# Gathering an expert's tokens as quarter rows and turning them on VectorE instead of TensorE

## The chip, the cores and the metric

The kernel runs on one core of a Trainium2 chip. The metric is the device time of one execution in microseconds (us), as the median of the runs shown. The engines that matter here are TensorE (PE in the profile; PEld is its weight load), VectorE (DVE), ScalarE (ACT), GpSimd (POOL, whose queue issues the gathers), and SyncE (SP, whose queue issues the weight loads). All transfers run on the core's 16 DMA engines.

## The reference

Three layers on 512 tokens of 1024 features in fp32. The first is a gated linear attention mixer followed by a mixture of experts, the second a Fourier and attention layer, the third a recurrent (RG-LRU) layer. The change lies in the mixture of experts and in the step that prepares its input:

```python
h = modulate(rmsnorm(h, norm_mlp_w[l]), sh2, sc2)        # 512 tokens x 1024
logits = xt @ w_router + b_router                        # top 4 of 32 experts for each token
def expert_block(args):                                  # one expert's tokens at a time
    gu = xblk @ w_gu[e] + b_gu[e]                        # 1024 x 2048
    gate, up = jnp.split(gu, 2, axis=-1)
    gate = jnp.minimum(gate, SWIGLU_LIMIT)
    up = jnp.clip(up, -SWIGLU_LIMIT, SWIGLU_LIMIT)
    act = (up + 1.0) * gate * jax.nn.sigmoid(SWIGLU_ALPHA * gate)
    return act @ w_down[e] + b_down[e]                   # 1024 x 1024
```

## The kernel before

**The norm step.** For each of the four blocks of 128 tokens, VectorE writes the normalised rows to `xnt` (`normalise`, L1252), TensorE turns them for the router, and GpSimd's queue stores them as rows of 1024 features in DRAM (`xn_scratch`, L1202). ScalarE squares the rows, takes the root and modulates half of the turned block (`square`, `modulate`).

**The experts.** Experts run one after the other, each with room for 96 tokens (`CAP`). Weights come through a ring of 12 slots of 1 MiB in SBUF: 8 tiles of `w_gu` and 4 of `w_down` for each expert, 12 MiB. SyncE's queue issues a load as soon as the semaphore `used` says that TensorE has left the slot (L1540). TensorE computes in column groups of 32: `gate_up` (L1774) makes, for each of 8 weight tiles, 12 matmuls of 512 columns (three groups of 32 tokens by four quarters of the columns, each split in two instructions as fp32), and a last set of 12 for the bias in bf16. `down` (L1754, L1759) does the same for the second product, one expert late.

One pass of the loop, `block_step(e)`, does this on TensorE, in this order: `gate_up` of expert e, its bias matmuls, the turning of the gathered tokens of expert e + 1 (`pe_turn`, L1458, eight transposes from `xe` into PSUM), `down` of expert e - 1, and the four small matmuls of `pe_ids` (L1448) that make the row numbers of expert e + 3 from a one-hot matrix. There are 32 passes; the first has no `down`. The loop's other engines:

- VectorE: reads the row numbers into `idx` (`dve_ids`, L1441), makes the one-hot matrix of the expert after (`dve_onehot`, L1437), then, once the bias matmuls are done, gate, up, their product and the 32x32 block transpose of the result (L1644 to L1658).
- GpSimd: waits for the row numbers and for both halves of the turning (L1505), then issues the gather of the next expert (`pool_gather`, L1492): one indirect transfer of 96 rows of 4 KB into partitions 0 to 95 of `xe`. A row number that is out of bounds moves nothing.
- ScalarE: the sigmoid (L1588), then eight modulations from PSUM into `xeT` (`act_modulate`, L1499), then the copies of `down`'s result (L1598, L1600) and its stores to `y_scratch` (L1604, L1607).

`gate_up` of expert e + 1 waits for all eight modulations. Ahead of the loop stands a chain for the first expert: one-hot, `pe_ids`, `idx`, gather, turning, modulation. SyncE loads three copies of the bias to 32 partitions each (L1521), waits for the first gather and then issues the six weight loads that have slots (L1529).

A last block of code serves experts with over 96 tokens, from a list that the kernel makes (`extra_blocks`).

## Time and profile before

| | before |
|---|---|
| median of 3 runs | 2387.15 us (2386.14 to 2388.25) |
| the profiled execution's own time | 2389.86 us |
| its span in the trace | 2387.9 us |
| granted TensorE clock, mean over the span | 0.971 |
| the experts, from the first `gate_up` to the last `down` | 364.6 to 1424 us |

Times below are in us from the start of the span unless marked ns. "Share" of the DMA engines is the mean busy share of 16 engines and can be a little over 1, since packets overlap. In a group row, the number after x is the count of instructions; [idle before <-X] is the engine's idle time and what ended it.

### The profile page before, as it was taken

What the parts mean: (1) busy time and instruction counts of PE and PEld (TensorE: products, weight loads), DVE (VectorE), ACT (ScalarE), POOL (GpSimd) and SP (SyncE); (2) the same over time, 40 slices, a digit from 0 to 9 for tenths busy, and PEclk for the clock granted to TensorE, in tenths of its full rate; (3) what the DMA queues carried; (4) which work ended last, traced back from release to release, by engine and by line L of the source; (5) the groups of instructions that cost most, each with busy time, mean ns of one, the idle gap of its engine ahead of it and who ended that gap; (6) DMA issues with size and microseconds to landing.
All of it is one profiled execution on the core that took longest, in us unless ns stands there. A gap on an engine that the chain in (4) does not pass through costs nothing. (4 is left out here: it accounts for less than half of the span.)

```text
span 2387.9 us, 35818 instructions
## 1 busy us (share of the span) xinstructions
PE 2249.2 (94%) x14707; PEld 930.6 (39%) x14707; DVE 681.3 (29%) x1157; ACT 486.8 (20%) x908; POOL 68.3 (3%) x105
## 2 busy tenths in 40 slices
PE   5999878999999999999999982999999998999998
PEld 2434532333333333333333330446445444444443
DVE  1133446111111111111111116003067103365633
ACT  2121212111110111101111111110016102456530
POOL 0000000000000000000000003000000000000000
PEclk8999888999999999999999995999999999999999
DMA  9138429999999999999999954422210121222100
GB/s 357 53 124 314 183 102 375 389 404 397 400 412 399 402 396 401 408 406 399 400 399 406 409 208 152 159 71 85 85 71 1 53 71 44 71 88 88 71 36 35
DMA packets 142023, 556.62 MB, mean 233 GB/s; under 512 B 17433, under 2 KB 32946, under 8 KB 108082
## 3 DMA queue, kind: packets, MB, share of 16 engines
q1 hardware_dynamic: 118662, 512.67, 55.3%
q0 software_dynamic: 9520, 30.29, 3.8%
q10 hardware_dynamic: 13788, 12.93, 1.6%
q8 instruction: 36, 0.59, 0.1%
q14 instruction: 17, 0.14, 0.0%
HBM read 535.77 MB, written 25.03 MB: 235 GB/s over the span
## 5 line engine op out<-in xcount | busy, mean ns | idle before, releaser
L1774 PE MATMUL ps<-ring,xeT 128*32 128x512 f32 x6144 | 670.4, 596 | 5.2 <-ACT xeT L1499 5.2
L1774 PEld LDWEIGHTS ps<-ring,xeT 128*32 128x32 f32 x6144 | 197.0, 110 | 450.3 <-issue 448.2
L1754 PE MATMUL ps<-ring,aT 128*32 128x512 f32 x2048 | 267.5, 594 | 1.0 <-ACT ysb L1600 1.0
L1644 DVE TENSOR_SCALAR gate<-ps 128x768 f32<-128x768 f32 x32 | 30.6, 958 | 606.7 <-PE ps L1774 606.7
L1588 ACT ACTIVATE sig<-gate 128x768 f32<-128x768 f32 x32 | 27.0, 845 | 702.1 <-DVE gate L1644 702.1
L360 PE MATMUL ps<-hT_late,ring 128*128 128x512 f32 x384 | 165.2, 592 | 1.7 <-PEq L2000 1.7
L1759 PE MATMUL ps<-ring,aT 128*32 128x256 f32 x2048 | 157.6, 379 | 0.0
L1759 PEld LDWEIGHTS ps<-ring,aT 128*32 128x32 f32 x2048 | 67.0, 110 | 152.7 <-issue 152.7
L2687 PE MATMUL ps<-hT_late,ring 128*128 128x512 f32 x256 | 110.6, 592 | 1.7 <-PEq L2446 1.7
L360 PE MATMUL ps<-ring,mT 128*128 128x512 f32 x256 | 110.1, 592 | 1.2 <-PEq L2253 1.2
L2700 PE MATMUL ps<-hT_late,ring 128*128 128x512 f32 x256 | 110.5, 592 | 0.0
L2738 PE MATMUL ps<-ring,mT 128*128 128x512 f32 x256 | 110.2, 592 | 0.0
L360 PEld LDWEIGHTS ps<-hT_late,ring 128*128 128x128 f32 x384 | 72.9, 190 | 93.3 <-issue 93.3
L1658 DVE STREAM_TRANSPOSE aT<-up 128x768 f32<-128x768 f32 x32 | 31.3, 978 | 232.2 <-PE ps L1759 232.2
L1499 ACT ACTIVATE xeT<-ps,mod 128x96 f32<-128x96 f32 x264 | 88.1, 437 | 1.6 <-PE ps L1458 1.6
L360 PE MATMUL ps<-ring,hT_late 128*128 128x512 f32 x192 | 82.6, 592 | 1.2 <-PEq L2110 1.2
L1754 PEld LDWEIGHTS ps<-ring,aT 128*32 128x32 f32 x2048 | 63.7, 110 | 42.7 <-ACT ysb L1600 1.1
L360 PEld LDWEIGHTS ps<-ring,mT 128*128 128x128 f32 x256 | 48.6, 190 | 62.7 <-issue 62.7
L2687 PEld LDWEIGHTS ps<-hT_late,ring 128*128 128x128 f32 x256 | 48.6, 190 | 62.7 <-issue 62.7
L2738 PEld LDWEIGHTS ps<-ring,mT 128*128 128x128 f32 x256 | 48.6, 190 | 61.2 <-issue 61.2
L2700 PEld LDWEIGHTS ps<-hT_late,ring 128*128 128x128 f32 x256 | 48.6, 190 | 61.2 <-issue 61.2
L360 PE MATMUL ps<-ring,hT 128*128 128x512 f32 x160 | 71.7, 598 | 0.0
(364 smaller groups left out, 1959.7 us busy)
## 6 DMA issues: line engine op xcount, KB each, us to landing
ring<-in_w_gu SPq DMA_DIRECT2D x256, 1024.0 KB, 12.1
ring<-in_w_down SPq DMA_DIRECT2D x128, 1024.0 KB, 12.8
ring<-in_even_w_in SPq DMA_DIRECT2D x18, 1024.0 KB, 6.2
ring<-in_w_ada SPq DMA_DIRECT2D x32, 512.0 KB, 6.5
ring<-in_odd_w_in SPq DMA_DIRECT2D x32, 512.0 KB, 5.5
ring<-in_w_ada SPq DMA_DIRECT2D x8, 1024.0 KB, 20.7
ring<-in_w_in SPq DMA_DIRECT2D x8, 1024.0 KB, 15.6
y_scratch<-ysb ACTq DMA_DIRECT2D x128, 64.0 KB, 5.0
```

The lines of the kernel that those rows point to most:

```text
L360: mm = nc.tensor.matmul(dst, left(k, w, kk), right(k, w, kk), start=first, stop=last)
L1499: nc.scalar.activation(xeT[:, k, 0:tokens_], ps[:, 6 + k // 4, at:at + tokens_], ACT.Identity, bias=mod2[:, k, 0:1], scale=mod2[:, KD + k, ...
L1588: nc.scalar.activation(sig[:, 0:W], gate[:, 0:W], ACT.Sigmoid, scale=1.702).then_inc(M.sig_ready, 1)
L1644: nc.vector.tensor_scalar(thirds(gate[:]), part_banks(0), 7.0, None, ALU.min).then_inc(M.gu_read, 1)
L1658: nc.vector.transpose(turned[:, 0:W], up[:, 0:W]).then_inc(M.aT_read, 1)
L1754: mm = nc.tensor.matmul(quad(Y0, 2 * q + n), acted(k, q), w[:, kk, n * BANK:(n + 1) * BANK], start=first, stop=last)
L1759: mm = nc.tensor.matmul(quad(Y0 + 1, c, 256), acted(k, 2), w[:, kk, c * 256:(c + 1) * 256], start=first, stop=last)
L1774: mm = nc.tensor.matmul(quad(q, c), left(q), part_columns(w, c), start=start, stop=stop)
L2687: mm = nc.tensor.matmul(bank(j.bank), w[:, b * P:(b + 1) * P], hT[:, k, :], start=k == 0, stop=k == KD - 1)
L2700: mm = nc.tensor.matmul(bank(j.bank), w[:, 512 + b * P:512 + (b + 1) * P], hT[:, k, :], start=k == 0, stop=k == KD - 1)
L2738: return nc.tensor.matmul(bank(j.bank), mT[:, k, t * P:(t + 1) * P], w[:, k % 2, h * BANK:(h + 1) * BANK], start=k == 0, stop=k == 2 * KD - 1)
```

## The change

The step that turns an expert's tokens moves from TensorE to VectorE, and the gather is laid out for it. VectorE transposes within blocks of 32 partitions and 32 columns. So the tokens are gathered as quarters of rows: quarter r of the token in slot 32q + s goes to partition 32r + s, columns 256q to 256q + 255. That takes three indirect transfers for an expert (q = 0, 1, 2), each of 128 quarter rows of 1 KB, with three columns of row numbers. One VectorE transpose of 128x768 then gives features on partitions. For the weights' rows to stay in natural order, the normalised rows are stored in another feature order (j, r, f to r, j, f), by ScalarE, which now writes a second copy of them in the norm step (`spread`).

The row numbers need the slot within 32 (`place`) and the third that it lies in (`third_of`), made by three VectorE steps ahead of the loop; `pe_ids` multiplies by six columns instead of two, masked by the third (`mine`, four more VectorE steps for each expert), and `dve_ids` takes two VectorE steps instead of one. The transposes leave TensorE, and the `used` signal that the first of them gave is given by the first matmul of `down`, or by `pe_ids` in the first pass. The waits follow: GpSimd waits for VectorE's transpose, ScalarE modulates from SBUF. The block for experts with over 96 tokens is changed in the same way. The core of the diff:

```diff
             def _(pool):
                 posm_zero.on(nc.gpsimd.memset(posm[:], 0.0))
                 for t in range(NT):
-                    pool.wait_ge(xn2_ready.sem, t + 1)
-                    xn2_stored.on(pool.dma_start(xn_dram[t * P:(t + 1) * P, :], xnt[:, t, :]), 16)
+                    pool.wait_ge(xq_ready.sem, t + 1)
+                    xn2_stored.on(pool.dma_start(xn_dram[t * P:(t + 1) * P, :], xq[t]), 16)
                 xn2_stored.wait(pool)
...
+                def spread(t):
+                    act.wait_ge(n2_mean.sem, 2 * t + 2)
+                    xq_ready.on(nc.scalar.activation(xq[t].rearrange("p (q j f) -> p j q f", q=4, f=QUAD),
+                                                     res[:, t, :].rearrange("p (j q f) -> p j q f", q=4, f=QUAD), ACT.Copy,
+                                                     scale=stat[:, 4 + t:5 + t]))
...
                 for t in range(NT):
                     square(t)
+                    spread(t)
                     modulate(t)
...
-        xe = sbuf("xe", [P, D], scope=moe_scope)
+        W = 3 * FF * QUAD // P
+        DQ = D // 4
+        xe = sbuf("xe", [P, W], scope=moe_scope)
+        xturned = sbuf("xturned", [P, W], scope=moe_scope)
+        place, third_of = (sbuf(f"{name}_of", [P, NT, E + 3], scope=moe_scope) for name in ("place", "third"))
+        placex, thirdx = (sbuf(f"{name}_extra", [P, NT, XB], scope=moe_scope) for name in ("place", "third"))
...
-        tokens = sbuf("tokens", [P, NT, 2], BF16, scope=moe_scope)
-        W = 3 * FF * QUAD // P
+        tokens = sbuf("tokens", [P, NT, 6], BF16, scope=moe_scope)
+        mine = sbuf("mine", [P, NT, 6], BF16, scope=moe_scope)
+        row = sbuf("row", [P, 3], scope=moe_scope)
         Q2 = slice(BANK, W)
         sel = sbuf("sel", [3 * E, P], BF16, scope=moe_scope)
-        idx = sbuf("idx", [P, 1], U32, scope=moe_scope)
+        idx = sbuf("idx", [P, 3], U32, scope=moe_scope)
...
-        iota1 = cst[:, C_IOTA1:C_IOTA1 + P]
+        slots = cst[:, C_SLOT:C_SLOT + P]
+        row_moved = signal("row_moved")
         ident3 = cst[0:3 * E, C_ID3:C_ID3 + E + 1]
...
-        def dve_onehot(dve, S, pos):
+        def split_places(step, pos, place_, third_):
+            step(nc.vector.tensor_scalar(third_, pos, float(QUAD), None, ALU.is_gt))
+            step(nc.vector.scalar_tensor_tensor(out=third_, in0=pos, scalar=2.0 * QUAD, in1=third_, op0=ALU.is_gt, op1=ALU.add))
+            step(nc.vector.scalar_tensor_tensor(out=place_, in0=third_, scalar=-float(QUAD), in1=pos, op0=ALU.mult, op1=ALU.add))
+        def dve_onehot(dve, S, place_, third_):
             for t in range(NT):
-                ins = nc.vector.tensor_scalar(onehot[:, t, 0:CAP], iota1[:, 0:CAP], pos(t), None, ALU.is_equal)
+                nc.vector.tensor_scalar(onehot[:, t, :], slots, place_(t), None, ALU.is_equal)
+                ins = nc.vector.scalar_tensor_tensor(out=mine[:, t, :], in0=cst[:, C_THIRD:C_THIRD + 6], scalar=third_(t),
+                                                     in1=tokens[:, t, :], op0=ALU.is_equal, op1=ALU.mult)
             ins.then_inc(S.onehot_ready, 1)
-        def dve_ids(dve, S):
-            nc.vector.tensor_scalar(idx[:], ps[:, IDS, 0:1], ps[:, IDS, 1:2], float(NONE), ALU.add, ALU.add).then_inc(S.ids_read, 1)
+        def dve_ids(dve, S, n):
+            nc.vector.tensor_reduce(row[:], ps[:, IDS, 0:6].rearrange("p (q c) -> p q c", q=3), AX.X, ALU.add) \
+                .then_inc(row_moved.sem, 1)
+            dve.wait_ge(row_moved.sem, n)
+            nc.vector.tensor_scalar(idx[:], row[:], cst[:, C_ROW:C_ROW + 1], None, ALU.add).then_inc(S.ids_read, 1)
...
         def pe_ids(pe, S, first=None):
             for t in range(NT):
-                mm = nc.tensor.matmul(ps[:, IDS, 0:2], onehot[:, t, :], tokens[:, t, :],
+                mm = nc.tensor.matmul(ps[:, IDS, 0:6], onehot[:, t, :], mine[:, t, :],
                                       start=t == 0, stop=t == NT - 1)
...
+        quarter_rows = xn_dram.rearrange("t (q n) -> (t q) n", q=4)
         def pool_gather(pool, S):
-            nc.gpsimd.indirect_dma_start(xe[0:CAP, :], None, xn_dram, bass.IndirectOffsetOnAxis(ap=idx[0:CAP, :], axis=0),
-                                         bounds_check=T - 1, oob_is_err=False).then_inc(S.gathered, 16)
-        def act_modulate(act, S, tokens_=CAP):
-            for k in range(KD):
-                at = (k % 4) * P
-                nc.scalar.activation(xeT[:, k, 0:tokens_], ps[:, 6 + k // 4, at:at + tokens_], ACT.Identity,
-                                     bias=mod2[:, k, 0:1], scale=mod2[:, KD + k, 0:1]).then_inc(S.xeT_read, 1)
+            for q in range(3):
+                nc.gpsimd.indirect_dma_start(xe[:, q * DQ:(q + 1) * DQ], None, quarter_rows,
+                                             bass.IndirectOffsetOnAxis(ap=idx[:, q:q + 1], axis=0),
+                                             bounds_check=4 * T - 1, oob_is_err=False).then_inc(S.gathered, 16)
+        def dve_turn(S):
+            nc.vector.transpose(xturned[:], xe[:]).then_inc(S.xT_done, 1)
+        def act_modulate(act, S):
+            for j in range(KD):
+                nc.scalar.activation(xeT[:, j, 0:CAP].rearrange("p (q s) -> p q s", q=3),
+                                     xturned[:].rearrange("p (q j s) -> p j q s", q=3, j=KD)[:, j], ACT.Identity,
+                                     bias=mod2[:, j, 0:1], scale=mod2[:, KD + j, 0:1]).then_inc(S.xeT_read, 1)
...
                 for part in range(3):
                     bgu_loaded.on(sp.dma_start(bgu[part * E:(part + 1) * E, :], A["b_gu"][0]), 16)
-                sp.wait_ge(M.gathered, 16)
+                sp.wait_ge(M.gathered, 48)
...
             def _(pool):
                 nc.gpsimd.memset(mark[:], 0.0).then_inc(M.marked, 1)
                 amat_zero.on(nc.gpsimd.memset(xe[:], 0.0))
+                amat_zero.on(nc.gpsimd.memset(xeT[:, :, CAP:], 0.0))
                 amat_zero.wait(pool)
-                for e in range(2):
-                    pool.wait_ge(M.ids_read, e + 1)
-                    if e:
-                        pool.wait_ge(M.xT_done, 2)
-                    pool_gather(pool, M)
+                pool.wait_ge(M.ids_read, 1)
+                pool_gather(pool, M)
+                pool.wait_ge(M.ids_read, 2)
+                pool.wait_ge(M.xT_done, 1)
+                pool_gather(pool, M)
                 def block_step(e):
                     pool.wait_ge(M.ids_read, e + 3)
-                    pool.wait_ge(M.xT_done, e * 2 + 4)
+                    pool.wait_ge(M.xT_done, e + 2)
                     pass_on(pool, M, e + 1)
                     pool_gather(pool, M)
...
-                    act.wait_ge(M.xT_done, e * 2 + 4)
+                    act.wait_ge(M.xT_done, e + 2)
                     act_modulate(act, M)
...
-                rest.on(nc.vector.memset(onehot[:, :, CAP:], 0.0))
-                rest.on(nc.vector.tensor_copy(tokens[:].rearrange("p t c -> p (t c)"), cst[:, C_TOK:C_TOK + 2 * NT]))
+                def list_step(ins):
+                    listing.on(ins)
+                    listing.wait(dve)
+                split_places(list_step, posm[:], place[:], third_of[:])
+                for q in range(3):
+                    rest.on(nc.vector.tensor_copy(tokens[:, :, 2 * q:2 * q + 2],
+                                                  cst[:, C_TOK:C_TOK + 2 * NT].rearrange("p (t c) -> p t c", t=NT)))
                 rest.wait(dve)
                 for e in range(3):
                     if e:
                         dve.wait_ge(M.ids_done, e)
-                    dve_onehot(dve, M, lambda t: posm[:, t, e:e + 1])
+                    dve_onehot(dve, M, lambda t: place[:, t, e:e + 1], lambda t: third_of[:, t, e:e + 1])
                     if e < 2:
                         dve.wait_ge(M.ids_done, e + 1)
                         if e:
-                            dve.wait_ge(M.gathered, 16 * e)
-                        dve_ids(dve, M)
+                            dve.wait_ge(M.gathered, 48)
+                        dve_ids(dve, M, e + 1)
+                        if e:
+                            dve.wait_ge(amat_zero.sem, buffers_zero)
+                            dve_turn(M)
...
                 def block_step(e, first):
                     dve.wait_ge(M.ids_done, e + 3)
-                    dve.wait_ge(M.gathered, e * 16 + 32)
-                    dve_ids(dve, M)
-                    dve_onehot(dve, M, lambda t: posm[:, t, bass.ds(e + 3, 1)])
+                    dve.wait_ge(M.gathered, e * 48 + 96)
+                    dve_ids(dve, M, e + 3)
+                    dve.wait_ge(M.xeT_read, e * 8 + 8)
+                    dve_turn(M)
+                    dve_onehot(dve, M, lambda t: place[:, t, bass.ds(e + 3, 1)], lambda t: third_of[:, t, bass.ds(e + 3, 1)])
                     dve.wait_ge(M.gate_done, e + 1)
...
@@ -1737,11 +1785,8 @@
                     if e:
                         pe.wait_ge(M.ids_read, e)
                     pe_ids(pe, M)
-                    if e == 0:
-                        pe.wait_ge(M.gathered, 16)
-                        pe_turn(pe, M.xT_done, xe, tokens_=CAP)
-                def down(e, m0, turn):
+                def down(e, m0, turn, final=False):
...
                             for q, n in pair_units():
                                 mm = nc.tensor.matmul(quad(Y0, 2 * q + n), acted(k, q), w[:, kk, n * BANK:(n + 1) * BANK],
                                                       start=first, stop=last)
+                                if first and q == n == 0 and not final:
+                                    mm.then_inc(stream.used, 1)
                             if last:
...
@@ -1787,18 +1835,16 @@
                         parted.wait(pe)
                     pe.wait_ge(M.sel_ready, e + 1)
                     gate_up(lambda q: sel[:, 0:QUAD], bparts[:], False, True).then_inc(M.gate_done, 1)
-                    pe.wait_ge(M.gathered, e * 16 + 32)
-                    pe_turn(pe, M.xT_done, xe, first=stream.used, tokens_=CAP)
                     if not first:
                         down(e, m0 + 8, turn)
                     pe.wait_ge(M.onehot_ready, e + 4)
                     pe.wait_ge(M.ids_read, e + 3)
-                    pe_ids(pe, M, first=None if first else stream.used)
+                    pe_ids(pe, M, first=stream.used)
...
-    cst[:, C_IOTA1:C_IOTA1 + P] = j + 1
+    cst[:, C_SLOT:C_SLOT + P] = j % 32 + 1
     cst[:, C_TRI:C_TRI + P] = p < j
...
     for t in range(NT):
-        cst[:, C_TOK + 2 * t:C_TOK + 2 * t + 1] = p
-        cst[:, C_TOK + 2 * t + 1] = P * t - NONE
+        cst[:, C_TOK + 2 * t:C_TOK + 2 * t + 1] = 4 * p
+        cst[:, C_TOK + 2 * t + 1] = 4 * (P * t - NONE)
     cst[:, C_RESET:C_RESET + T + TC] = np.arange(T + TC) % CHUNK != 0
     cst[:, C_XI:C_XI + XB] = np.arange(XB)
+    cst[:, C_THIRD:C_THIRD + 6] = np.arange(6) // 2
+    cst[:, C_ROW:C_ROW + 1] = 4 * NONE + p // 32
```


## Rows read from the trace of the kernel before

**Rows 1.** The page: busy time, mean ns of one, idle before.
```profile
PE 2249.2 (94%) x14707; PEld 930.6 (39%) x14707; DVE 681.3 (29%) x1157; ACT 486.8 (20%) x908; POOL 68.3 (3%) x105
...
L1658 DVE STREAM_TRANSPOSE aT<-up 128x768 f32<-128x768 f32 x32 | 31.3, 978 | 232.2 <-PE ps L1759 232.2
```

**Rows 2.** Windows in the experts: busy by engine, PEclk, DMA share, GB/s.
```profile
500.00:600.00 100.00, 100.00 (x1052) 34.64 (x1048) 16.92 (x33) 12.88 (x33) 3.48 (x6) 1.00 1.01 400
...
1200.00:1300.00 100.00, 100.00 (x1052) 34.61 (x1044) 16.91 (x33) 12.88 (x33) 3.47 (x6) 1.00 1.02 403
```

**Rows 3.** Timeline of TensorE around one pass: start us, us, instructions.
```profile
909.34 0.88 PE L1458 MATMUL ps<-cst,xe 96*128 96x96 f32 x8
910.15 1.06 PE L1754 MATMUL ps<-ring,aT 128*32 128x512 f32 x8
...
920.61 0.25 PE L1448 MATMUL ps<-tokens,onehot 128*128 128x2 bf16 x4
...
942.18 0.88 PE L1458 MATMUL ps<-cst,xe 96*128 96x96 f32 x8
```

**Rows 4.** DMA issues, us to landing: 394:400, 500:600, 1250:1350.
```profile
ring<-in_w_gu SPq DMA_DIRECT2D x1, 1024.0 KB, 6.7
...
ring<-in_w_gu SPq DMA_DIRECT2D x24, 1024.0 KB, 8.9
...
ring<-in_w_gu SPq DMA_DIRECT2D x24, 1024.0 KB, 15.0
```

**Rows 5.** Windows of one pass: while its gather's packets move, and the rest.
```profile
915.00:920.00 5.00, 5.00 (x68) 1.98 (x64) 0.00 (x0) 0.00 (x0) 0.00 (x0) 1.00 1.02 309
920.00:948.00 28.00, 28.00 (x292) 9.50 (x288) 5.63 (x11) 4.29 (x11) 1.15 (x2) 1.00 1.02 418
```

**Rows 6.** DMA, ten passes (900 to 1228.4): packets, MB, share of 16 engines.
```profile
q10 hardware_dynamic: 3840, 3.94, 3.4%
q0 software_dynamic: 1120, 2.83, 2.9%
...
xe<-xn_scratch,idx POOLq DMA_INDIRECT x10, 8.8
```

**Rows 7.** Windows elsewhere: bias loads, input loads, gathers of the next stage.
```profile
355.00:357.00 2.00, 0.16 (x4) 0.07 (x3) 0.94 (x5) 0.00 (x0) 0.61 (x1) 0.50 1.02 217
10.00:14.00 4.00, 0.00 (x0) 0.00 (x0) 0.00 (x0) 1.28 (x1) 0.00 (x0) 1.00 1.02 392
...
1440.00:1443.00 3.00, 3.00 (x4) 1.15 (x4) 0.75 (x1) 0.00 (x0) 0.00 (x0) 0.50 0.97 399
```

**Rows 8.** Timeline ahead of the first gate_up: the chain of the first expert.
```profile
354.03 0.81 DVE L1437 TENSOR_SCALAR onehot<-cst,posm 128x96 bf16<-128x96 f32 x4
...
355.20 0.22 DVE L1441 TENSOR_SCALAR idx<-ps 128x1 uint32<-128x1 f32 x1 [0.36 <-PE ps L1448]
...
356.39 1.02 POOL L1492 DMA_INDIRECT xe<-xn_scratch,idx  x1 [2.43 <-DVE idx L1441]
...
360.30 1.54 PE L1458 MATMUL ps<-cst,xe 96*128 96x96 f32 x8 [5.14 <-DMA xe<-xn_scratch,idx]
...
361.88 2.68 ACT L1499 ACTIVATE xeT<-ps,mod 128x96 f32<-128x96 f32 x8 [1.55 <-PE ps L1458]
...
377.35 0.29 DVE L1689 SCALAR_TENSOR_TENSOR sgT<-cst,sgT 128x128 f32<-128x128 f32 x1
```

**Rows 9.** Timeline, later: start of the second expert, and ScalarE in one pass.
```profile
393.65 0.64 PE L1774 MATMUL ps<-ring,xeT 128*32 128x512 f32 x4 [3.81 <-ACT xeT L1499]
...
911.19 2.67 ACT L1499 ACTIVATE xeT<-ps,mod 128x96 f32<-128x96 f32 x8
```

**Rows 10.** Timeline of the norm step, last block: ScalarE and VectorE.
```profile
341.10 1.06 ACT L1211 ACTIVATE kT<-res 128x1024 f32<-128x1024 f32 x1 [8.49 <-DVE res L1243]
...
345.33 1.50 ACT L1219 ACTIVATE ring<-ps,mod 128x128 f32<-128x128 f32 x4 [2.19 <-PE ps L1342]
```

**Rows 11.** The instructions on the tile idx: ns min/median/max, first and last start.
```profile
L1492 POOL DMA_INDIRECT xe<-xn_scratch,idx x34: 966/971/1025, 356.4 to 1403.7; - x34
```

More of the change, by code:

```diff
@@ L426, in build @@
         posm = sbuf("posm", [P, NT, E + 3])
-        posx = sbuf("posx", [P, NT, XB])
         wk = sbuf("wk", [P, NT, TOPK])
@@ L1122, in build @@
         parts = kT[:].rearrange("p a n -> p (a n)")[:, D:D + T]
+        xq = [a.rearrange("p h n -> p (h n)") for a in (vtok[:, 0:2, :], vtok[:, 2:4, :], vtok[:, 4:6, :], ptok[:, 0:2, :])]
         rt = sgT[:].rearrange("p h n -> p (h n)")
@@ L1188, in build @@
         posm_zero = signal("posm_zero")
+        xq_ready = signal("xq_ready")
         with nc.Block() as block:
@@ L1452, in pe_ids, with pe_turn @@
             mm.then_inc(S.ids_done, 1)
-        def pe_turn(pe, signal_, src, first=None, n=KD, tokens_=P):
-            for k in range(n):
-                at = (k % 4) * P
-                mm = nc.tensor.transpose(ps[:, 6 + k // 4, at:at + tokens_], src[0:tokens_, k * P:(k + 1) * P],
-                                         ident[0:tokens_, 0:tokens_])
-                if k == 0 and first:
+        def pe_turn(pe, signal_, src, first):
+            for k in range(KD):
+                mm = nc.tensor.transpose(ps[:, 6 + k // 4, (k % 4) * P:(k % 4 + 1) * P], src[:, k * P:(k + 1) * P], ident)
+                if k == 0:
                     mm.then_inc(first, 1)
-                if k % 4 == 3 or k == n - 1:
+                if k % 4 == 3:
                     mm.then_inc(signal_, 1)
@@ L1658, in block_step @@
                     nc.vector.transpose(turned[:, 0:W], up[:, 0:W]).then_inc(M.aT_read, 1)
-                def step(ins):
-                    listing.on(ins)
-                    listing.wait(dve)
+                step = list_step
                 def weights_and_rows():
@@ L1717, in _ @@
                 listing.wait(dve)
-                step(nc.vector.tensor_reduce(posx[:], indw, AX.X, ALU.add))
+                posx = ind.rearrange("p x e -> p (x e)")[:, 0:NT * XB].rearrange("p (t x) -> p t x", t=NT)
+                step(nc.vector.tensor_reduce(posx, indw, AX.X, ALU.add))
                 step(nc.vector.scalar_tensor_tensor(
-                    out=posx[:], in0=xval[:, 1:2, :].to_broadcast([P, NT, XB]), scalar=-float(CAP), in1=posx[:],
+                    out=posx, in0=xval[:, 1:2, :].to_broadcast([P, NT, XB]), scalar=-float(CAP), in1=posx,
                     op0=ALU.mult, op1=ALU.add))
+                split_places(step, posx, placex[:], thirdx[:])
                 step(nc.vector.tensor_copy(xlist[:, 0:XB], xval[:, 0, :]))
@@ L1800, in _ @@
                     block_step(i + 1, 8, i, False)
-                down(E, 8 + 12 * (E - 1), 0)
+                down(E, 8 + 12 * (E - 1), 0, final=True)
                 stream.taken = end_moe
@@ L1911, in body @@
                     pe.wait_ge(X.act_ready, i + 1)
-                    pe_turn(pe, X.aT_done, up, first=x_used)
+                    pe_turn(pe, X.aT_done, up, x_used)
                     pe.wait_ge(X.aT_read, i * 2 + 2)
```

24 lines of the change are left out of this document (12 added, 12 removed).

## The prediction

> **What bounds the kernel now.** I read the page first. TensorE is busy for 2249 us of the span, every other engine for under a third of it [rows 1]. The windows of 100 us inside the experts say more: TensorE is busy for all of each window at full granted clock, and at the same time the 16 DMA engines have a share of 1.01 to 1.02 and move 400 to 403 GB/s [rows 2]. So there are two candidates for the bound, and the first question is which of them ends last in a pass of the expert loop.
>
> The timeline of one pass answers it for TensorE [rows 3]: from one turning (909.34) to the next (942.18) is 32.84 us, and the queue of matmuls has no hole. The landing times of the weight loads answer it for the DMA [rows 4]: a load takes 6.7 us from issue to landing at the start of the loop, 8.9 us around 550, 15.0 us around 1300. The DMA engines are therefore late by a little more after each pass (6.1 us in 750 us, or 22.8 passes: 0.27 us a pass), and nothing waits for them, because the ring absorbs it. A slot that is left is needed again eleven twelfths of a pass later, 30.1 us, and 15.0 is well below that. TensorE is the bound, the DMA engines stand right behind it. What is taken from TensorE can be had only as far as the ring has room.
>
> What a pass asks of the DMA engines, in parts: twelve loads of 1 MiB are 12.58 MB, the stores 3.94 MB in ten passes, together 12.98 MB [rows 6]. Between gathers the core moves 418 GB/s [rows 5], so this takes 31.04 us. The gather is 0.283 MB a pass [rows 6] (about 69 rows of 4 KB), 0.68 us at that rate. But while its packets move, for about 5 us, the core moves only 309 GB/s [rows 5]: 5 x (418 - 309) / 418 = 1.30 us more are lost. The sum, 33.02 us against a pass of 32.84, agrees with the lag of 0.27 to within 0.1. So the gather is dear less for its bytes than for what it does to the others while it runs.
>
> **The change, part by part.**
>
> *The transposes leave TensorE.* From the first transpose to the first matmul of `down` is 910.15 - 909.34 = 0.81 us [rows 3]. The bound from the other side is the group's busy time, 0.88. The matmul behind it waits for things done long before. In the first pass nothing is gained: TensorE then idles 3.81 us for the modulations [rows 9], whose chain starts at the bias matmuls, not at the turning. 31 passes remain: 31 x 0.81 = 25.1 us less (up to 27.3). The new pass is 32.03 us.
>
> *`pe_ids` with six columns for two.* Four matmuls take 0.25 us with two columns [rows 3]; four more columns each are priced at nothing (at most 31 x 0.1 = 3 us, if every small matmul grew by 25 ns).
>
> *VectorE's additions in a pass*: a transpose of 128x768 (0.98 us [rows 1]), four small masks, one small reduction (each about `idx`'s 0.22 [rows 8]), some 2.1 us. VectorE is under a fifth busy [rows 2], and these stand right behind `pe_ids`, 20 us ahead of the next bias matmuls that VectorE waits for. Nothing on the path. Behind them on VectorE stands only the one-hot matrix, which TensorE wants 30 us later.
>
> *GpSimd*: three gathers of about 1.0 us issue time instead of one. They can be issued some 4 us after `pe_ids`, where the old one was issued after the turning, and they are needed at the next `idx`, 30 us later: 3 us of issue and 8.8 us of landing [rows 6] leave 17 us. Without that cover each us would cost 31.
>
> *ScalarE* modulates from SBUF; the eight took 2.67 us and ended at 913.9 [rows 9], 6.9 us ahead of the next `gate_up` (920.8, right behind `pe_ids` [rows 3]). It stays covered, with 0.8 less. Exposed it is only for the first two experts; a different price from SBUF would show there, within 1 us.
>
> *The norm step*: a copy of 128x1024 on ScalarE for each block of tokens, priced by the square of the same size, 1.06 us [rows 10]. It fits in the 2.19 us in which ScalarE waits for TensorE's turning. Zero; at most 1 us if the spread access pattern doubled it.
>
> *The chain of the first expert* is exposed, and it grows [rows 8]. Added: three steps of 128x140 ahead of the one-hot (0.29 each for 128x128, with hand-overs 1.0); two more small copies (0.4); four masks beside the one-hots, which take 0.81 for four (0.4); the reduction and its wait (0.3); two more gathers issued one after the other (2 x 1.02, with gaps 2.3). Taken away: TensorE's turning of 1.54 for VectorE's 0.98 (-0.5). Sum +3.9, taken as +4; bounds 3 and 6 (all small steps at 0.3, and hand-overs doubled). The six loads behind the first gather (L1529) start as much later, but so does TensorE's demand for them.
>
> *The gathers on the DMA engines* is the part that the trace does not show. Bytes stay 0.283 MB; in packets of 1 KB they cost at most what the stores of 1 and 2 KB rows cost, 3.94 MB in 3.4% of 16 x 328.4 us, that is 353 GB/s [rows 6]: 0.80 us. The disturbance is the open term, between 0 and three times 1.30. What makes it? A queue of GpSimd's beside SyncE's is not enough: at 10 to 14, GpSimd's loads of the input rows run beside weight loads, into all 128 partitions, at 392 GB/s. Into few partitions it is different: the bias loads, 32 partitions each, run at 217 GB/s at a share of 1.02, with no gather beside them at 355. And gathers of 128 rows, alone, run at 399 [rows 7]. The old gather fills at most 96 partitions, mostly the lowest 69; the new ones go to all 128. So I take the value near 0: a pass then asks 31.04 + 0.80 = 31.84 us of the DMA engines, just under 32.03, and the lag no longer grows.
>
> The Trainium skill, DMA: Bandwidth & Descriptors, The descriptor swizzle, says that in a transfer over 128 partitions each engine's writes go to the partitions behind one port of its own, and the same page's Back-pressure in remote DMA that a saturated port holds up the engines behind it (told there for transfers between cores). Our two windows at 217 and 392 GB/s are what that would look like; that it explains the gather's 309 no row shows. By it the disturbance would be 0, and the sum the one I give.
>
> **Sum.** -25.1 + 4 = -21.1 us. The profiled execution has a span of 2387.9 and a time of 2389.86; it would give 2368.8. From the median of the runs, 2387.15, comes 2366.
>
> **How much of the lag is free.** At the start a load lands in 6.7 us [rows 4]; with the shorter pass the limit is 29.4. So 22.7 us of lag can grow over 31 passes before TensorE waits: a pass may ask 32.03 + 0.73 of the DMA engines. If it asks g us more than 32.03, the loop gets 31g - 22.7 longer. All of the gain is gone at 31g = 22.7 + 21.1, g = 1.41: a disturbance of 32.03 + 1.41 - 31.84 = 1.60 us a pass, barely more than the old one.
>
> **The rivals.**
>
> *A, the disturbance stays 1.30.* It goes with the bytes or with the mixture of scattered rows, not with the partitions. For it: the old gather's cost is real and its cause not proven. Against: the loads at 10 to 14. A pass asks 33.14 of the DMA, g = 1.11, 34.4 - 22.7 = 11.7 us are given back as waits of `gate_up` and `down` for weight tiles in the last third of the loop. Time 2366 + 12 = 2378.
>
> *B, slower: each of the three transfers disturbs as the one did.* The place is the loop, the mechanism a cost for each indirect transfer or for each of its row numbers (384 for 96). For it: a dip of 5 us for 0.3 MB looks like something other than bytes. Against: GpSimd's direct loads, which have as many packets. At three times, 3.90, g = 3.71 and 115 - 22.7 = 92 us come back: 2458. At twice, 2.60, g = 2.41: 52 us, 2418. It decides from 1.60 on, 0.53 for each transfer.
>
> The Trainium skill, DMA: Bandwidth & Descriptors, Anatomy of one DMA and Rules for kernel authors, speaks against the change here: a transfer has some 2.0 us fixed, and many small ones should be made one. Were these 2.0 us time of the DMA engines, two more transfers would ask 4.0 us more a pass, an estimate from that page, and by it beside A's 1.30 g would be 5.1 and the time near 2502. The windows speak for latency instead.
>
> *C, another small mishap*: the first expert's chain at its upper bound together with a gather or a modulation that is late in some passes, 5 to 15 us given back: 2371 to 2381. The gathers run only for the 32 experts: 34 issues [rows 11], two of them ahead of the loop, so the block for over 96 tokens does not run.
>
> **How the numbers follow.** The forecast 0.60, A 0.15, B 0.18, C 0.07. The forecast's own range is 2361 (0.88 for each turning, a chain of 3) to 2371. The range for 8 in 10 takes in A and C, and the start of B, where the disturbance lies between 1.3 and 1.9: 2360 to 2394. What a measurement can tell from no change here is 0.2%, 4.8 us: same is 2382.4 to 2391.9, which lies between A and B. So faster 0.75 (the forecast, most of A and C), same 0.06, slower 0.19.
>
> **What would show it.** In the timeline of a pass `down` follows the bias matmuls directly, and the pass is 32.0 us. The windows of 5 us while the gathers' packets move show over 390 GB/s (forecast), about 310 (A), or a longer dip (B). The landing time of the weight loads stays under 12 us to the end of the loop (forecast), or rises to 29 and then TensorE's waits name a DMA of the ring (A, B). The first `gate_up` starts near 368.6. VectorE's and ScalarE's new work shows as busy time with no new waits behind it. Wrong makes me above all a dip that does not go away.

## The result, and the profile after

The changed kernel takes 2359.45 us (median of 4 runs, 2357.59 to 2360.21), the kernel before in the same rounds 2387.7 us (2386.14 to 2388.48). The ratio is 0.9883 with a 95% interval from 0.987 to 0.9895: between 25 and 31 us less, 28.25 in the medians. 21.1 were forecast; the direction was right and the forecast gain a quarter too small, so that the time came out 0.55 us below the range's low end.

The page of the changed kernel, in the columns of [rows 1]; the last rows are DMA issues (KB each, us to landing):

```profile
PE 2215.9 (94%) x14443; PEld 907.7 (39%) x14443; DVE 738.2 (31%) x1371; ACT 501.8 (21%) x912; POOL 141.1 (6%) x174
...
L1522 POOL DMA_INDIRECT xe<-xn_scratch,idx x102 | 105.8, 1037 | 44.3 <-issue 37.0
L1533 ACT ACTIVATE xeT<-xturned,mod 128x96 f32<-128x96 f32 x264 | 97.9, 456 | 3.6 <-DVE xturned L1528 3.6
...
ring<-in_w_gu SPq DMA_DIRECT2D x256, 1024.0 KB, 8.3
```

TensorE is busy for 33 us less, VectorE for 57 more and GpSimd for 73 more. The new work of VectorE (and ScalarE's modulation from SBUF) has no large wait behind it: of ScalarE's 264 modulations together only 3.6 us were waited for. TensorE's timeline over one pass:

```profile
892.88 0.83 PE L1822 MATMUL ps<-bparts,sel 96*32 96x512 bf16 x12
893.53 1.04 PE L1799 MATMUL ps<-ring,aT 128*32 128x512 f32 x8
...
903.97 0.26 PE L1476 MATMUL ps<-mine,onehot 128*128 128x6 bf16 x4
...
924.78 0.83 PE L1822 MATMUL ps<-bparts,sel 96*32 96x512 bf16 x12
```

`down` now follows the bias matmuls directly. From one bias group to the next are 31.90 us (31.895 over many passes); before, they were 32.84 [rows 3]. From `down` to `pe_ids` it is 10.44 us, before 10.46: six columns instead of two cost nothing.

The windows, in the columns of [rows 2]: two of 100 us, and three of 2 us in which the three gathers' packets move (issued at 907.23, 908.55 and 909.86; they land 6.2 us after their issue in the median):

```profile
500.00:600.00 100.00, 100.00 (x1056) 33.59 (x1048) 21.80 (x51) 13.77 (x33) 9.68 (x12) 1.00 1.02 414
...
1200.00:1300.00 100.00, 100.00 (x1052) 33.55 (x1048) 21.81 (x51) 13.76 (x33) 9.68 (x12) 1.00 1.02 415
909.00:911.00 2.00, 2.00 (x24) 0.55 (x20) 0.00 (x0) 0.00 (x0) 1.56 (x2) 1.00 1.06 421
911.00:913.00 2.00, 2.00 (x24) 0.65 (x20) 0.00 (x0) 0.00 (x0) 0.00 (x0) 1.00 1.02 410
913.00:915.00 2.00, 2.00 (x24) 0.61 (x20) 0.00 (x0) 0.00 (x0) 0.00 (x0) 1.00 1.07 420
```

The dip to 309 GB/s [rows 5] is gone, and the loop moves 414 and 415 GB/s in the two long windows. Accordingly the weight loads land in 8.2 us around 550 and in 8.1 around 1300, where it was 8.9 and 15.0 [rows 4]; in between they rise a little (8.8 around 950, 9.0 from 1200 to 1300). Here are both windows, and ten passes of GpSimd's queue (packets, MB, share) against [rows 6]:

```profile
ring<-in_w_gu SPq DMA_DIRECT2D x26, 1024.0 KB, 8.2
...
ring<-in_w_gu SPq DMA_DIRECT2D x24, 1024.0 KB, 8.1
...
q0 software_dynamic: 1440, 2.83, 2.3%
```

The first expert's chain, in a timeline of all engines (0.82 for `third_of` to 22.93 for the first `gate_up`), and the wait ahead of the second expert:

```profile
349.37 0.10 POOL L1582 MEMSET mark<- 128x1 f32 x1 [7.55 <-POOLq L1191]
...
349.41 0.82 DVE L1452 TENSOR_SCALAR third_of<-posm 128x140 f32<-128x140 f32 x1 [0.32 <-PEq L1191]
...
354.45 1.09 POOL L1522 DMA_INDIRECT xe<-xn_scratch,idx  x1 [3.97 <-DVE idx L1469]
...
355.84 1.04 POOL L1522 DMA_INDIRECT xe<-xn_scratch,idx  x1 [0.30 <-issue]
357.19 1.00 POOL L1522 DMA_INDIRECT xe<-xn_scratch,idx  x1 [0.30 <-issue]
...
359.74 0.97 DVE L1528 STREAM_TRANSPOSE xturned<-xe 128x768 f32<-128x768 f32 x1
...
360.75 2.97 ACT L1533 ACTIVATE xeT<-xturned,mod 128x96 f32<-128x96 f32 x8 [3.60 <-DVE xturned L1528]
...
363.77 22.93 PE L1822 MATMUL ps<-ring,xeT 128*32 128x512 f32 x192 [1.38 <-ACT xeT L1533]
...
392.34 8.13 PE L1822 MATMUL ps<-ring,xeT 128*32 128x512 f32 x60 [4.81 <-ACT xeT L1533]
```

From the experts' first instruction (the memset of `mark`) to the first `gate_up`: 363.77 - 349.37 = 14.40 us. In the profile of before it was 352.98 to 364.62, 11.64.

### The profile page after: what moved, and what is told of

The parts are those of the page before. It is cut to its first block and busy times, and to the rows that moved or that the text cites. A ratio compares the mean times of both kernels' runs of the same rounds, so it can differ in the third digit from the quotient of the medians.

```text
span 2357.4 us, 35769 instructions
## 1 busy us (share of the span) xinstructions
PE 2215.9 (94%) x14443; PEld 907.7 (39%) x14443; DVE 738.2 (31%) x1371; ACT 501.8 (21%) x912; POOL 141.1 (6%) x174
## 5 line engine op out<-in xcount | busy, mean ns | idle before, releaser
L1522 POOL DMA_INDIRECT xe<-xn_scratch,idx x102 | 105.8, 1037 | 44.3 <-issue 37.0
L1533 ACT ACTIVATE xeT<-xturned,mod 128x96 f32<-128x96 f32 x264 | 97.9, 456 | 3.6 <-DVE xturned L1528 3.6
```

Source lines behind the costliest of these rows:

```text
L1522: nc.gpsimd.indirect_dma_start(xe[:, q * DQ:(q + 1) * DQ], None, quarter_rows, bass.IndirectOffsetOnAxis(ap=idx[:, q:q + 1], axis=0), boun ...
L1533: nc.scalar.activation(xeT[:, j, 0:CAP].rearrange("p (q s) -> p q s", q=3), xturned[:].rearrange("p (q j s) -> p j q s", q=3, j=KD)[:, j], ...
```

## The experiments

Eleven kernels ran. "The pass" below is the time from one group of bias matmuls to the next; "lag" is by how much the time of gate_up's weight loads from issue to landing grows with each pass. Each lag is read from one trace.

**turn8 and turn16: the price of a turning.** The changed kernel gets eight (sixteen) transposes of a constant back on TensorE, between the bias matmuls and `down`.

```diff
                     gate_up(lambda q: sel[:, 0:QUAD], bparts[:], False, True).then_inc(M.gate_done, 1)
+                    pe.wait_ge(M.gathered, e * 48 + 96)
+                    for k in range(8):
+                        nc.tensor.transpose(ps[:, 6 + k % 8 // 4, (k % 4) * P:(k % 4) * P + CAP],
+                                            cst[0:CAP, (k % 8) * P:(k % 8 + 1) * P], ident[0:CAP, 0:CAP])
                     if not first:
                         down(e, m0 + 8, turn)
```

> The changed kernel with eight transposes put back on TensorE between the bias matmuls and down (of constants, results unused). Theory 1: a turning costs its own 0.81 us and 0.13 us more at the boundary behind the bias matmuls, so the pass is 32.84 us again and the time rises by 31 x 0.945 = 29 us, to about 2389. Theory 2: a turning costs 0.81 as forecast, and the rest of the gain came from elsewhere: pass 32.70, 25 us more, about 2384.5.

> The same with sixteen transposes. If the extra is a price of the boundary, paid once: pass 31.90 + 0.13 + 2 x 0.81 = 33.65 us, 54 us more than the changed kernel, about 2414. If each eight transposes cost 0.945: pass 33.79, 59 us more, about 2418. The weight loads then land in 7 us or less throughout, since the DMA engines have 1.7 us more a pass.

turn8: 2390.37 us, ratio 1.0011 (1.0001 to 1.002) to the kernel before; the pass is 32.84 again, as by theory 1. With the transposes alone all of the gain goes; the 2.7 us above the kernel before agree with what the first two experts lose, below. turn16: 2410.88, 1.0096 (1.0079 to 1.0112), pass 33.495. TensorE in one pass of turn8:

```profile
907.35 0.83 PE L1822 MATMUL ps<-bparts,sel 96*32 96x512 bf16 x12
908.11 0.88 PE L1840 MATMUL ps<-cst 96*128 96x96 f32 x8
908.92 1.07 PE L1799 MATMUL ps<-ring,aT 128*32 128x512 f32 x8
```

and of turn16:

```profile
918.02 0.83 PE L1822 MATMUL ps<-bparts,sel 96*32 96x512 bf16 x12
918.78 1.54 PE L1840 MATMUL ps<-cst 96*128 96x96 f32 x16
920.25 1.07 PE L1799 MATMUL ps<-ring,aT 128*32 128x512 f32 x8
```

The first eight cost 32.84 - 31.895 = 0.945 us a pass, the second eight 33.495 - 32.84 = 0.655. So 0.29 us do not go with their number: they are paid once, for having such a group there at all. A price paid once was the first reading, but with 0.13 and 0.81 us instead of 0.29 and 0.655: turn16 was to take 54 or 59 us more than the changed kernel, and took 51.4.

**turn8_late: is it the place?** The same eight stand behind `down`, right ahead of `pe_ids`, which uses the full array too.

> turn8 with the eight transposes moved behind down, right ahead of the small matmuls of the row numbers. In turn8 the first eight cost 0.945 us a pass and in turn16 the second eight 0.655, so 0.29 belongs to the two boundaries between matmuls of 32 columns and of 128. Theory 1 (boundary): the row numbers' matmuls already stand between two such boundaries, so the eight cost only their own 0.65: pass 32.55, time 2380. Theory 2 (the 0.29 is the start of any group with a wait of its own): pass 32.84, 2389.

2382.97 us, 0.9979 (0.9969 to 0.9988). The pass is 32.60, 0.705 more than without them:

```profile
907.17 0.83 PE L1822 MATMUL ps<-bparts,sel 96*32 96x512 bf16 x12
907.83 1.04 PE L1799 MATMUL ps<-ring,aT 128*32 128x512 f32 x8
...
918.26 0.88 PE L1842 MATMUL ps<-cst 96*128 96x96 f32 x8
918.98 0.25 PE L1476 MATMUL ps<-mine,onehot 128*128 128x6 bf16 x4
```

Beside a group that uses 128 columns of the array anyway (the 128 in 128*128), the extra is 0.05 us; inserted between two groups of 32 columns (96*32, 128*32) it is 0.29. Both places have the same wait, so it is the change of form on both sides that costs. The time lies between the two forecasts of 2380 and 2389; the pass is nearly that of theory 1 (32.55).

**rows_96: the old gather in the new kernel.** One transfer, 96 partitions, whole rows of 4 KB; row numbers and waits follow. VectorE turns the first 768 columns of what comes, so the experts get features in wrong places; the work stays the same but for one small VectorE step ahead of the loop.

```diff
-            for q in range(3):
-                nc.gpsimd.indirect_dma_start(xe[:, q * DQ:(q + 1) * DQ], None, quarter_rows,
-                                             bass.IndirectOffsetOnAxis(ap=idx[:, q:q + 1], axis=0),
-                                             bounds_check=4 * T - 1, oob_is_err=False).then_inc(S.gathered, 16)
+            nc.gpsimd.indirect_dma_start(xe[0:96, :], None, xn_dram, bass.IndirectOffsetOnAxis(ap=idx[0:96, 0:1], axis=0),
+                                         bounds_check=T - 1, oob_is_err=False).then_inc(S.gathered, 16)
```

> The changed kernel with the old gather: one indirect transfer of 96 rows of 4 KB for each expert, into partitions 0 to 95; VectorE still turns (the features that reach the experts are then not in their right places). Theory 1 (the old gather disturbs the other transfers, 1.30 us a pass): the DMA engines need about 33.1 us a pass against 31.9, the landing time rises by 1.2 us a pass to 29, then TensorE waits for weight tiles: 31 x 1.2 - 21 = 16 us back, less 2.6 us for two gathers not issued ahead of the first expert: about 2373. Windows of 5 us at the gathers at about 310 GB/s. Theory 2 (the disturbance hung on the place of the gather beside the down loads and not on its form): landing times flat near 9 us, 2357.

2362.05 us, 0.9893 (0.9876 to 0.9909). Three windows in which the gather's packets move:

```profile
910.00:912.00 2.00, 2.00 (x24) 0.65 (x20) 0.00 (x0) 0.00 (x0) 0.00 (x0) 1.00 1.03 393
912.00:914.00 2.00, 2.00 (x24) 0.62 (x20) 0.00 (x0) 0.00 (x0) 0.00 (x0) 1.00 1.04 314
914.00:916.00 2.00, 2.00 (x24) 0.55 (x20) 0.00 (x0) 0.00 (x0) 0.00 (x0) 1.00 1.03 399
```

The landing of the loads, around 480 and around 1300 (gate_up's and then `down`'s):

```profile
ring<-in_w_gu SPq DMA_DIRECT2D x11, 1024.0 KB, 10.2
...
ring<-in_w_gu SPq DMA_DIRECT2D x24, 1024.0 KB, 19.5
ring<-in_w_down SPq DMA_DIRECT2D x13, 1024.0 KB, 23.9
```

The row of the waits of TensorE's weight loads that names the ring, over the whole loop (us in total, times, longest):

```profile
PEld ps L1821 <- DMA ring<-in_w_gu: 10.4, 16, 1.2
```

The dip is back, and the lag is 0.66 us a pass until gate_up's loads are at 19.5 us, around 925. TensorE first waits only in the 27th to 29th of the 31 passes (32.57, 32.82 and 32.17 us, together 1.9 more than three of 31.895), and then the loop is nearly over. So the disturbance is real, and its price in this kernel was 2 us of time rather than the 12 of rival A (the forecast for this run was 2373, or 2357 without a disturbance); up to 925 a pass asked the DMA engines for 31.895 + 0.66 = 32.56 us, not 33.14, an estimate from the lag.

From 925 on gate_up's landing time stays at 19.5 to 20.6 while `down`'s goes on to 25 (around 1150). By then SyncE's issues are late themselves: four loads of `down` take 15.62 us to issue, in rows_128 (next) at the same place 8.19. The time from issue to landing then no longer shows the whole lag. What holds the issues back no row shows.

```profile
1151.50 15.62 SPq L1575 DMA_DIRECT2D ring<-in_w_down  x4
```

and in rows_128:

```profile
1150.39 8.19 SPq L1575 DMA_DIRECT2D ring<-in_w_down  x4
```

**rows_128: the same rows, but the transfer names 128 partitions** (`xe[0:128, :]`, `idx[0:128, 0:1]`), with 32 row numbers out of bounds.

> As rows_96, but the transfer names all 128 partitions; the last 32 row numbers are out of bounds and move nothing, so the same rows go to the same partitions as in rows_96. Theory 1 (what disturbs is how 96 rows are dealt to the 16 engines): no dip, landing times flat near 9 us, time about 2357, as the changed kernel less two issues. Theory 2 (what disturbs is 4 KB rows into the lowest 69 partitions, or rows read at scattered places): as rows_96, about 2373, landing up to 29.

2359.97 us, 0.9884 (0.9867 to 0.99), 2.1 us under rows_96 in the medians, with ranges that overlap. There is no dip (the windows from 909 to 919 show 414 to 430 GB/s), and GpSimd's queue takes 2.3% of the engines' time, as in the changed kernel, against 2.8% in rows_96. But the landing still rises, around 550 and around 950:

```profile
ring<-in_w_gu SPq DMA_DIRECT2D x26, 1024.0 KB, 8.5
...
ring<-in_w_gu SPq DMA_DIRECT2D x24, 1024.0 KB, 12.5
```

Half of the lag, 0.32 us a pass, is left, without any dip. Each theory holds in one half, so there are two parts.

**rows_128_spread and rows_96_spread: who carries the rows.** In rows_128 the 69 or so real rows sit in the lowest partitions, so that, if each DMA engine serves partitions of its own, some engines have rows to move and others none. Here the filled slots are dealt over all partitions:

```diff
-    cst[:, C_SLOT:C_SLOT + P] = np.where(j < CAP, j + 1, -1)
+    cst[:, C_SLOT:C_SLOT + P] = np.where(j % 4 < 3, 32 * (j % 4) + j // 4 + 1, -1)   # 128
+    cst[:, C_SLOT:C_SLOT + P] = np.where(j < CAP, 32 * (j % 3) + j // 3 + 1, -1)     # 96
```

> rows_128 with only the constant of slot numbers changed: slot s of an expert no longer sits in partition s but the 96 slots are spread over all 128 partitions, three of every four. In rows_128 the 64 or so real rows all lie in partitions 0 to 63. Theory 1 (balance: half of the DMA engines carry all of the gather, and a weight load lands with its slowest engine): the landing time, which rose by 0.32 us a pass in rows_128, now stays within 8 to 10 us as in the changed kernel. Theory 2 (the rest of the lag belongs to 4 KB rows or to one transfer instead of three): it rises to 15 us as before. Time about 2359 by both.

> rows_96 with the slots spread over its 96 partitions, two real rows in three. Theory 1 (balance explains all of the old gather's disturbance): the rise of 0.66 us a pass goes, landing times stay near 9 us, gather packets of 4 KB take 160 ns instead of 199. Theory 2 (96 partitions do not divide among the engines as the weight loads do, so that engines meet at the same partitions): packets stay near 200 ns, and the landing time still rises by 0.3 us a pass or more, to at least 15.

rows_128_spread: 2359.89 us, 0.9883 (0.9867 to 0.99), and loads that land in the same time around 550 and 950:

```profile
ring<-in_w_gu SPq DMA_DIRECT2D x25, 1024.0 KB, 7.7
...
ring<-in_w_gu SPq DMA_DIRECT2D x24, 1024.0 KB, 7.7
```

rows_96_spread: one run, 2360.47 us. The dip is there, in one of the windows of 2 us:

```profile
913.00:915.00 2.00, 2.00 (x24) 0.65 (x20) 0.00 (x0) 0.00 (x0) 0.00 (x0) 1.00 1.02 339
```

And the lag is there, by the landing times around 550 and 950:

```profile
ring<-in_w_gu SPq DMA_DIRECT2D x26, 1024.0 KB, 8.9
...
ring<-in_w_gu SPq DMA_DIRECT2D x24, 1024.0 KB, 14.1
```

The four kernels differ in two choices. Between the windows around 550 and 950 lie 12.5 passes, and the lag in them is 0.62 us a pass with 96 partitions and the lowest first (11.9 to 19.6), 0.32 with 128 and the lowest first, 0.42 with 96 dealt out, and 0 with 128 dealt out. So the 96 partitions cost 0.30 to 0.42 us a pass and the uneven load 0.20 to 0.32. The larger figure of each pair is against the lag of 0, where the DMA engines may have had time to spare, so it can be too small. From 950 to the window of 1200 to 1300 the rise is slower (0.28 in rows_128, 0.31 in rows_96_spread). The duration of the gather's packets goes with the partitions alone: over the passes from 900 to 1219 one of 4 KB takes in the mean 201 ns in rows_96 and 189 in rows_96_spread, and 159 in both kernels with 128. What makes them longer no row shows. The changed kernel has neither: its three gathers name 128 partitions, and each filled slot has quarters in all four groups of 32.

**before_128: the kernel before, with its gather over 128 partitions** (`xe[:]`, `idx[:]` for `xe[0:CAP, :]`, `idx[0:CAP, :]`).

> The kernel before with one thing changed: the gather names all 128 partitions instead of 96, the last 32 row numbers out of bounds. Theory 1 (how 96 rows are dealt to the engines disturbs): the dip of 5 us at 309 GB/s goes, weight loads land in under 9 us to the end of the loop, and the time stays at 2387, since TensorE is the bound there (pass 32.84). Theory 2 (place of the gather beside the down loads): dip and rise to 15 us stay. A second reading: the experts' block started at 353.0 in the profile of before and at 347.8 to 349.8 in five profiles of kernels made from the changed one. If that is chance, this kernel may start anywhere from 348 to 353; if it belongs to the change, near 353.

2389.66 us, 1.001 (1.000 to 1.0019): no gain, since the pass is TensorE's, 32.84. The lag is gone (7.8 us around 950, 12.8 before). The disturbance had cost the kernel before nothing; it had only used up the ring. But theory 1 was wrong on the dip: from 908 to 914 the core still moves only 330 to 363 GB/s, now at a share a little under 1, and loses nothing by it.

```profile
912.00:914.00 2.00, 2.00 (x32) 0.85 (x28) 0.00 (x0) 0.00 (x0) 0.00 (x0) 1.00 0.97 330
```

The uneven load is still there, as in rows_128; a pass that asked some 31.895 + 0.32 = 32.2 us would fit into 32.84 without a lag. By that estimate the 96 partitions cost the kernel before 33.1 - 32.2, some 0.9 us a pass, some three times what they cost in rows_96. So the price is not the same in every kernel; whether the gather's other place in the pass makes the difference was not tested.

**quarter_96: the changed kernel with its three gathers cut to 96 partitions**, which leaves out the last quarter of each row.

> The changed kernel with its three gathers cut to 96 partitions each (the quarter of the features that goes to partitions 96 to 127 is left out). Theory 1 (the deal of 96 rows): the disturbance comes back although there are fewer bytes: gather packets longer than 161 ns for 4 KB, landing times rising from 8 to 12 or more over the loop. Theory 2 (long rows): flat at 8 to 9 us. The time is 2359 either way, as the ring holds it.

One run, 2361.36 us. The loads land in 7.8 us around 550 and in 10.7 around 950 (8.2 and 8.8 in the changed kernel): a lag of 0.23 us a pass for 0.05, with a quarter fewer bytes. From 950 to the window of 1200 to 1300 it is 0.11. Theory 1 asked for longer packets as well, and they are not longer: one of 4 KB takes 161 ns in the mean, as in the changed kernel. So the lag of this form, in one run, has another look than that of rows_96, and its cause is not shown.

**one_gather: only the first of the three**, so that two thirds of each expert's features are not fetched.

> The changed kernel with only the first of the three gathers (tokens beyond an expert's first 32 are left out). The chain of the first expert gets shorter by the two issues, 2.7 us, and the experts start 2.7 us earlier after their block's start (14.4 to 11.7); the pass stays 31.90. Time 2357. Rival: the landing of the last of three is hidden behind something else in the chain, and less than 1 us comes back.

2360.11 us, 0.9884 (0.9867 to 0.99): the same time as with three. The first chain is 12.67 us instead of 14.40. Its part from the issue of the gather to VectorE's turning:

```profile
354.95 1.09 POOL L1522 DMA_INDIRECT xe<-xn_scratch,idx  x1 [4.30 <-DVE idx L1469]
...
358.27 0.97 DVE L1528 STREAM_TRANSPOSE xturned<-xe 128x768 f32<-128x768 f32 x1
```

3.32 us, against 359.74 - 354.45 = 5.29 with three: where they are exposed, a further gather costs 0.98 us, less than the 1.37 from one issue to the next, since the last of three is back sooner after its issue. In the profile 1.7 us of chain come back, between the 2.7 forecast and the rival's 1; in the time nothing shows. In the loop, where the pass stays 31.895, two more cost nothing.

**mod_first: ScalarE modulates ahead of the sigmoid in the first pass**, which gives the same output.

```diff
+                    if first:
+                        act.wait_ge(M.gate_done, 1)
+                        act.wait_ge(M.xT_done, e + 2)
+                        act_modulate(act, M)
```

> The changed kernel with ScalarE's order turned round in the first pass alone: the eight modulations ahead of the sigmoid, as soon as the bias matmuls are done. TensorE's idle time ahead of the second expert falls from 4.8 to about 3.0 us, everything else as it is: 1.8 us less, 2357.6. Rival: the second expert then waits for its first weight tiles instead, and nothing is gained.

2358.53 us, 0.9883 (0.9867 to 0.99). TensorE ahead of the second expert:

```profile
385.74 0.82 PE L1827 MATMUL ps<-bparts,sel 96*32 96x512 bf16 x12
...
389.83 10.49 PE L1827 MATMUL ps<-ring,xeT 128*32 128x512 f32 x80 [3.08 <-ACT xeT L1533]
```

From bias to second expert 4.09 us for 5.81 in the changed kernel: 1.7 us less in the profile, which the times can't tell from nothing.

## Why the prediction was right in kind and short in size

**What bounds.** Right. TensorE sets the pass, and turn8 brings the whole 0.945 us back with TensorE work alone.

**The transposes leave TensorE.** This is the step that failed, the term that was mis-sized: 0.81 us a turning was predicted, with the busy time of 0.88 as the bound from above, and 0.945 were measured, 31 x 0.945 = 29.3 us for 25.1. I had taken the price as the time from the first transpose to the first `down`, and had not looked at what stood ahead of it, in the kernel before:

```profile
908.57 0.83 PE L1774 MATMUL ps<-bparts,sel 96*32 96x512 bf16 x12
```

From there to the first transpose (909.34) are 0.77 us. In turn8 the bias matmuls hold the array for 908.11 - 907.35 = 0.76 us before the transposes can start, and in the changed kernel for 893.53 - 892.88 = 0.65 before `down`, 0.11 less. Behind stand the 0.81 from transposes to `down`, of which eight transposes need 0.655 (turn16); the last 0.02 or so are in the first group of `down` (1.07 us for 1.04). Neither the start-to-start time nor the busy time of a group is an upper bound of what leaves with it.

The Trainium skill, TensorEngine Tiling (Array Packing), Key Properties, says that a change of tiling mode, unlike a change of tile, drains TensorE. The runs agree in direction: 0.29 us for a group of full width between groups of 32 columns, 0.05 where its neighbour is of full width already. Whether it is a drain, no row shows.

**The chain of the first expert.** Predicted +4 (3 to 6). Measured +2.8 against the profile of before, +2.4 against before_128, whose chain takes 11.97: a little under the lower bound, the second term that was mis-sized. By parts: the steps up to the first gather took 354.45 - 349.37 = 5.08 us for 3.41, +1.7 where 2.1 were summed; the gathers, from issue to turning, 5.29 for 3.91 [rows 8], +1.4 for 2.3; turning and modulation 363.77 - 359.74 = 4.03 for 4.32, -0.3 for -0.5. The gathers were the overpriced part, since a first quarter gather is back sooner (3.32 us) than one of whole rows (3.91), and two more cost 1.97 instead of 2.3 (one_gather).

**The wait ahead of the second expert** grows from 3.81 us [rows 9] to 4.81, the way from bias to `gate_up` by 0.3: eight modulations from SBUF take 2.97 us (360.75) for 2.67. It had been allowed for within 1 us.

**The other steps** were right. `pe_ids`: nothing. VectorE and GpSimd stay covered. The norm step's extra copy shows no delay: from the step's first instruction to the experts' it is 61.0 us, before 61.1.

**The sum** of what was measured: -29.3 + 2.6 + 0.3 = -26.4 us, within the interval of 25 to 31. From the experts' first instruction to the end of the span the profiles show 2008.0 us for 2034.9, 26.9 less (26.6 against before_128). So the steps account for 5.3 of the 7.2 us by which the gain was larger than forecast; the other 1.9 are within the interval and have no step of their own. By the measured steps alone the time would be 2361.3. (The forecast's own low end of 2361 does not follow from its terms either: 2387.15 - 27.3 + 3 is 2362.9.) The two profiled executions differ by more, 2387.9 - 2357.4 = 30.5 us, because in that of before the experts began at 352.98, in that of after at 349.37. In the other profiles they begin anywhere from 347.8 to 352.1, in before_128, which is the same kernel up to there, at 348.9, and in rows_128_spread at 352.0. Those 3.6 us are no effect of the change.

**The gathers on the DMA engines.** The value near 0 was right, and so was what it was taken for: "into few partitions it is different". It was half of the cause. The other half, the uneven load, had not been thought of. The 1.30 us was on weaker ground: it was worked out from the dip, and before_128 has a dip without a lag. That its sum agreed with the lag of before does not prove it. Even so the 31.84 us that a pass was to ask came close: the landing rises by 0.05 us a pass (8.2 around 550, 8.8 around 950), so a pass asks some 31.94, an estimate. The Trainium skill, DMA: Bandwidth & Descriptors, The descriptor swizzle, gives for a transfer over 128 partitions eight partitions to each engine. By that deal the rows of rows_128 fall to half of the engines and a few more, and those of rows_128_spread to all alike; the lags of 0.32 and 0 agree, though no row here names the engine of a packet. The section tells nothing of 96.

**The rivals.** A fell in both parts: the disturbance did not stay, and had it stayed, it would have cost 2 us and not 12: the new kernel with the old gather asks for 32.56 us a pass. The dip is shorter there (314 GB/s for 2 us) and the pass asks 0.6 us less than A's 33.14. Why it is shorter was not settled; the gather is issued at another point of the pass. A's limit of 29.4 us of landing was too high on the other side: TensorE waited when gate_up's loads were at some 20 and down's at 25. The issues were late by then, and the landing time counts from the issue. B fell: three transfers disturb less than one, and one_gather, with one, is no faster. With two more gathers a pass a weight load still lands in 8.1 us around 1300. The fixed 2.0 us of a transfer in the Trainium skill, DMA: Bandwidth & Descriptors, Anatomy of one DMA, therefore are not time of the DMA engines here, as the prediction had supposed for its 2502. C did not show; the one thing late is 0.3 us once.

## What to carry to other kernels

The price of work that leaves an engine is the difference of two whole periods, not the length of its own rows: look at how long the group ahead of it holds the engine, above all where TensorE goes from 32 columns to full width and back. Where TensorE and the DMA engines are nearly level, read the landing times at several places of a loop before and after; a dip of GB/s by itself is no loss (before_128 moves 330 to 363 GB/s from 908 to 914 and has no lag), and once the issues are late, a landing time that stays flat does not show that all is well (rows_96). And where the DMA engines have no time to spare, let a gather name all 128 partitions and deal its real rows over them, with row numbers out of bounds for the rest; in the kernels here that shortened no time by more than 2 us.

## What was not expected of the hardware

- A group of TensorE at full width costs 0.29 us more than its own work when it stands between groups of 32 columns, and 0.05 beside one of full width (turn8, turn16, turn8_late).
- An indirect transfer over 96 partitions beside loads over 128 makes these late by 0.30 to 0.42 us a pass more than one over 128 with at least a quarter of its rows out of bounds; the uneven placing of some 69 rows makes them late by another 0.20 to 0.32 (rows_96, rows_128 and their spread forms, from 550 to 950; in the kernel before the 96 partitions cost more). The share of GpSimd's queue for the same 2.83 MB falls from 2.8% to 2.3%, by a sixth.
- Rows of 1 KB had no price beside rows of 4 KB: 2.3% of the engines' time for 2.83 MB in the changed kernel and in rows_128 alike, in 1440 packets both.
